# The last GEMM of a two-block transformer kernel: seven block products for eight

## The reference

```
def conv_ffn(h, w_up, conv_w, conv_b, w_down):
    u = causal_depthwise_conv(h @ w_up, conv_w, conv_b)
    gate, up = jnp.split(u, 2, axis=-1)
    return (jax.nn.silu(gate) * up) @ w_down
...
        x = x + conv_ffn(rms_norm_2(x, ffn_norm[layer]), ffn_w_up[layer], ffn_conv_w[layer],
                         ffn_conv_b[layer], ffn_w_down[layer])
```

## Time and profile before

| | |
|---|---|
| median of 3 runs | 1476.79 us |
| the profiled execution: span | 1474.6 us |
| around the span (median less span) | 2.2 us |
| TensorE busy | 1464.9 us, 99% |
| DVE, ACT, POOL busy | 824.7, 587.4, 207.0 us |
| mean granted TensorE clock | 0.998 |
| the stage of conv_down | from 1351.5 us to 1471.5 us of the span |

### The profile page before, as it was taken

One profiled execution on the slowest core, in us unless ns is written; L12 is line 12 of the kernel. 1 busy time (PEld: TensorE's weight loads), 2 busy tenths in 40 slices (PEclk: granted clock), 3 DMA queues, 4 the chain that ended last, 5 costly groups with the idle time before them and its releaser, 6 DMA issues.

```text
span 1474.6 us, 21796 instructions
## 1 busy us (share of the span) xinstructions
PE 1464.9 (99%) x8300; PEld 1221.1 (83%) x8300; DVE 824.7 (56%) x1264; ACT 587.4 (40%) x913; POOL 207.0 (14%) x193
## 2 busy tenths in 40 slices
...
GB/s 176 200 86 107 38 2 143 114 87 86 1 86 86 114 86 113 85 103 97 85 114 86 57 87 86 86 95 104 33 30 86 86 88 111 85 110 74 103 113 57
DMA packets 149743, 132.31 MB, mean 90 GB/s; under 512 B 6300, under 2 KB 133532, under 8 KB 149668
## 3 DMA queue, kind: packets, MB, share of 16 engines
...
q10 hardware_dynamic: 1056, 0.00, 0.0%
...
## 4 chain that ended last, share of the span: by engine, by line
PE 97%; DVE 1%; POOL 1%; DMA 0%; issue 0%; ACT 0%; SPq 0%; DVEq 0%; POOLq 0%
PE ps L2013 28%; PE ps L2015 28%; PE ps L2014 28%; PE ps L2448 3%; PE ps L2537 1%; PE ps L2555 1%; PE ps L2638 1%; PE ps L2647 1%; PE ps L2458 1%; PE ps L486 1%; POOL x_t L743 1%; DMA arena<-in_x 0%; PE ps L2479 0%; PE ps L2706 0%; PE ps L2707 0%; PE ps L2374 0%
## 5 line engine op out<-in xcount | busy, mean ns | idle before, releaser
L2013 PE MATMUL ps<-a_hi,w_hi 128*128 128x512 f32 (+2 forms) x1576 | 588.6, 373 | 3.7 <-DVE a_lo L1631 1.3
L2015 PE MATMUL ps<-a_hi,w_lo 128*128 128x512 f32 (+2 forms) x1576 | 583.3, 370 | 0.0
L2014 PE MATMUL ps<-a_lo,w_hi 128*128 128x512 f32 (+2 forms) x1576 | 583.1, 370 | 0.0
L819 ACT ACTIVATE w_hi<-raw 128x2048 fp32r<-128x2048 f32 x116 | 221.9, 1913 | 330.1 <-PE ps L2015 328.3
L2013 PEld LDWEIGHTS ps<-a_hi,w_hi 128*128 128x128 f32 (+1 forms) x1576 | 296.2, 188 | 60.1 <-DVE a_lo L1453 4.1
L1338 DVE TENSOR_TENSOR w_lo<-raw,w_hi 128x2048 fp32r<-128x2048 f32 x96 | 219.9, 2290 | 220.7 <-ACT w_hi L819 220.1
L2015 PEld LDWEIGHTS ps<-a_hi,w_lo 128*128 128x128 f32 (+1 forms) x1576 | 296.2, 188 | 51.9
L2014 PEld LDWEIGHTS ps<-a_lo,w_hi 128*128 128x128 f32 (+1 forms) x1576 | 296.3, 188 | 50.7 <-issue 0.7
L691 POOL TENSOR_TENSOR w_lo<-raw,w_hi 128x2048 fp32r<-128x2048 f32 x22 | 101.4, 4609 | 435.7 <-ACT w_hi L819 408.0
L1844 DVE TENSOR_TENSOR arena<-ps,rstd 128x512 f32<-128x512 f32 x88 | 60.1, 689 | 164.1 <-PE ps L2015 159.1
L2013 PE MATMUL ps<-w_hi,a_hi 128*128 128x512 f32 x368 | 144.0, 391 | 0.0
...
## 6 DMA issues: line engine op xcount, KB each, us to landing
raw<-in_w_gate_up SPq DMA_DIRECT2D x44, 512.0 KB, 4.7
raw<-in_ffn_w_up SPq DMA_DIRECT2D x44, 512.0 KB, 4.7
raw<-in_attn_w_in SPq DMA_DIRECT2D x36, 512.0 KB, 4.5
raw<-in_w_in SPq DMA_DIRECT2D x24, 512.0 KB, 4.7
raw<-in_w_down SPq DMA_DIRECT2D x22, 512.0 KB, 4.1
raw<-in_ffn_w_down SPq DMA_DIRECT2D x22, 512.0 KB, 3.9
raw<-in_w_mem_kv SPq DMA_DIRECT2D x16, 512.0 KB, 4.4
raw<-in_w_out SPq DMA_DIRECT2D x8, 512.0 KB, 4.0
```

The costliest lines, as they stand in the source:

```text
L819: act.activation(w_hi[:, ch.next_slot, :], raw[:, ch.next_slot, :], ACT.Copy).then_inc(weights_hi, 1)
L2013: pe.matmul(dst, s_hi, m_hi, start=start, stop=False, skip_group_check=across)
L2014: pe.matmul(dst, s_hi, m_lo, start=False, stop=False, skip_group_check=across)
L2015: return pe.matmul(dst, s_lo, m_hi, start=False, stop=stop, skip_group_check=across)
```

## The change

conv_down is replaced by a scheme after Strassen and Winograd. Of each pair of hidden tiles and its 256 rows of w_down, let A11, A12 be the first 256 tokens of the first and the second tile, A21, A22 the other 256 tokens, and W11, W12, W21, W22 the weights (first index the tile, second the half of the columns). With S1 = A21 + A22, S2 = S1 - A11, S3 = A11 - A21, S4 = A12 - S2, T1 = W12 - W11, T3 = W22 - W12, T2 = T3 + W11, T4 = W21 - T2 there are seven products in place of eight: P1 = A11 W11, P2 = A12 W21, P3 = S4 W22, P4 = A22 T4, P5 = S1 T1, P6 = S2 T2, P7 = S3 T3. The four quarters of the output are P1+P2, P1+P6+P5+P3, P1+P6+P7+P4 and P1+P6+P7+P5. Each product is 256 tokens by 512 columns over 128 of depth, and fills two PSUM banks.

Since PSUM has 8 banks, depth is run through twice (`STEPS`, 22 steps): steps 0 to 10 sum P1, P5, P7, P6 over the 11 pairs (24 matmuls a step), steps 11 to 21 then P2, P3, P4 on top of P1, P5, P7 in their banks (18 a step). At the turn ACT copies P1, P5, P7 out (`staged`), DVE adds P6 to P1 and that to three quarters (`join`), POOL adds P5 and P7 to one of them.

The work by engine: SP loads three quarters of w_down a step of the first run (256 KB each) and stores T2 to DRAM; in the second run it loads T2 and two quarters. The buffers are `raw`, `x_t` (free when the residual is turned) and a part of `arena` (free when the hidden matrix is whole). DVE makes T1 with T3 (128x1024), T2, T4 (128x512) and the weights' remainders (128x2048, then 128x1536). ACT makes all high parts. POOL makes S2 for each pair once (`basis`, two of 128x256, during conv_up), S1 and S3 or S4 (`sides`, 128x256) and the left operand's remainders (`sides_lo`), which were DVE's. Some semaphores of the start are joined into one (`x_norm`, `rel_moved`) with the same counts; the work there is the same. In `products` a triple is the first column of the side, the quarter and the first bank.

```diff
...
+        t2_dram = nc.dram_tensor("t2_dram", [FT // 2, 128, 512], F, kind="Internal").ap()
...
+        PAIRS_K = FT // 2
+        BUFFERS = (raw[:, :, :].rearrange("p a (q n) -> p (a q) n", n=512), x_t, region(16384, 8, 512))
...
+            def products(self):
+                if self.first:
+                    return ((512, 2, 0), (0, 0, 4), (256, 1, 6), (768, 3, 2))
+                return ((0, 1, 0), (512, 2, 4), (256, 0, 6))
+        STEPS = [Step(c) for c in range(2 * PAIRS_K)]
+        P1_BANK, P5_BANK, P7_BANK, P6_BANK = 0, 4, 6, 2
+        staged_1, staged_5, staged_7 = BUFFERS[0][:, 6:8, :], BUFFERS[1][:, 6:8, :], BUFFERS[2][:, 6:8, :]
...
+            def load_quarters(t):
+                if t.c == 0:
+                    sp.wait_ge(weights_split, TOTAL + CREDIT)
+                elif t.c == 1:
+                    sp.wait_ge(out_turned, KT)
+                elif t.c == 4:
+                    sp.wait_ge(hidden_written, 2 * CREDIT + 2 * FT)
+                else:
+                    sp.wait_ge(weights_split, TOTAL + CREDIT + t.before + 1)
+                if t.first:
+                    parts = ((2, 0, 0), (4, 0, 1), (5, 1, 1))
+                else:
+                    parts = ((1, 1, 0), (2, 1, 1))
+                    sp.wait_ge(t2_stored, 16 * (min(t.before, PAIRS_K - 1) + 1))
+                    sp.dma_start(t.q[:, 3, :], t2_dram[t.pair]).then_inc(rows_loaded[t.buffer], 16)
+                for to, k, n in parts:
+                    sp.dma_start(t.q[:, to, :], w_down[t.pair, k][:, n * 512:n * 512 + 512])\
+                      .then_inc(rows_loaded[t.buffer], 16)
+            def store_t2(t):
+                sp.wait_ge(quarter_sums, t.sums_done)
+                if t.c:
+                    sp.wait_ge(t2_stored, 16 * t.c)
+                sp.dma_start(t2_dram[t.pair], t.q[:, 3, :]).then_inc(t2_stored, 16)
+            load_quarters(STEPS[0])
+            load_quarters(STEPS[1])
+            for t in STEPS:
+                if t.first:
+                    store_t2(t)
+                if t.c + 2 < 4:
+                    load_quarters(STEPS[t.c + 2])
+                elif t.c == 2:
+                    load_quarters(STEPS[4])
+                    load_quarters(STEPS[5])
+                elif 3 <= t.c and t.c + 3 < len(STEPS):
+                    load_quarters(STEPS[t.c + 3])
...
+            def basis(t):
+                pool.wait_ge(hidden_written, 2 * CREDIT + FT + 2 * t.pair + 2)
+                a11, a21, a22 = t.hidden[:, 0:256], t.hidden[:, 256:512], t.hidden[:, 768:1024]
+                pool.tensor_tensor(a21, a21, a22, ALU.add).then_inc(basis_made, 1)
+                pool.wait_ge(basis_made, 2 * t.pair + 1)
+                pool.tensor_tensor(a21, a21, a11, ALU.subtract).then_inc(basis_made, 1)
+            def sides(t):
+                if t.c >= 3:
+                    pool.wait_ge(hidden_split, PAIRS_K + 2 * (t.c - 2))
+                pool.wait_ge(basis_made, 2 * (t.pair + 1))
+                a11, s2, a12, a22 = (t.hidden[:, n:n + 256] for n in (0, 256, 512, 768))
+                if t.first:
+                    pool.tensor_tensor(t.sums[:, 0:256], s2, a11, ALU.add).then_inc(side_sums, 1)
+                    pool.tensor_tensor(t.sums[:, 256:512], a22, s2, ALU.subtract).then_inc(side_sums, 1)
+                else:
+                    pool.tensor_tensor(t.sums, a12, s2, ALU.subtract).then_inc(side_sums, 1)
+            def sides_lo(t):
+                for n, (of, cols) in enumerate(t.side_parts()):
+                    pool.wait_ge(hidden_hi, PAIRS_K + 2 * t.c + n + 1)
+                    pool.tensor_tensor(t.side(a_lo)[:, cols], of, t.side(a_hi)[:, cols].bitcast(F), ALU.subtract)\
+                        .then_inc(hidden_split, 1)
+            for t in STEPS[:PAIRS_K - 1]:
+                basis(t)
+            sides(STEPS[0])
+            for t in STEPS:
+                if t.c == PAIRS_K - 4:
+                    basis(STEPS[PAIRS_K - 1])
+                if t.c + 1 < len(STEPS):
+                    sides(STEPS[t.c + 1])
+                sides_lo(t)
+                if t.c in (PAIRS_K + 5, PAIRS_K + 7):
+                    late = t.c - PAIRS_K - 5
+                    pool.wait_ge(product_joined, 4 + late // 2)
+                    pool.wait_ge(product_staged, 3)
+                    pool.tensor_tensor(out_quarter(1, 1), out_quarter(1, 1), staged_5 if late else staged_7, ALU.add)\
+                        .then_inc(product_joined, 1)
...
+            def sides_hi(t):
+                if t.c < 3:
+                    act.wait_ge(rows_free["conv_up"], t.c + 1)
+                elif t.c == 3:
+                    act.wait_ge(tile_done, G["conv_up"].signal_end)
+                else:
+                    act.wait_ge(tile_done, G["conv_up"].signal_end + t.c - 3)
+                for of, cols in t.side_parts():
+                    if of is t.sums:
+                        act.wait_ge(side_sums, t.sides_done)
+                    else:
+                        act.wait_ge(basis_made, 2 * (t.pair + 1))
+                    act.activation(t.side(a_hi)[:, cols], of, ACT.Copy).then_inc(hidden_hi, 1)
+            def quarters_hi(t):
+                act.wait_ge(quarter_sums, t.sums_done)
+                if t.c < 2:
+                    act.wait_ge(tile_done, G["conv_up"].signal_end - 2 + 2 * t.c)
+                else:
+                    act.wait_ge(tile_done, G["conv_up"].signal_end + t.c - 1)
+                act.activation(t.weight(w_hi), t.q[:, 0:t.many, :], ACT.Copy).then_inc(weights_hi, 1)
...
-                    first_rows_hi("conv_up", 2 * CREDIT + FT)
+                    sides_hi(STEPS[0])
+                    sides_hi(STEPS[1])
+                    quarters_hi(STEPS[1])
...
+                if ch.last_of_gemm:
+                    sides_hi(STEPS[2])
+                    quarters_hi(STEPS[2])
...
-            act.wait_ge(hidden_written, 2 * CREDIT + 2 * FT)
-            over_chunks(act, G["conv_down"], rows_hi)
+            for t in STEPS[3:]:
+                sides_hi(t)
+                if t.c == PAIRS_K + 1:
+                    staged(1, P1_BANK, staged_1)
+                    staged(2, P5_BANK, staged_5)
+                    staged(3, P7_BANK, staged_7)
+                quarters_hi(t)
...
+            def t1_and_t3(t):
+                loaded(t)
+                dve.tensor_tensor(t.q[:, 0:2, :], t.q[:, 4:6, :], t.q[:, 2:5:2, :], ALU.subtract).then_inc(quarter_sums, 1)
+            def t2(t):
+                dve.wait_ge(quarter_sums, t.sums_done - 1)
+                if t.before is not None:
+                    dve.wait_ge(t2_stored, 16 * (t.before + 1))
+                dve.tensor_tensor(t.q[:, 3, :], t.q[:, 1, :], t.q[:, 2, :], ALU.add).then_inc(quarter_sums, 1)
+            def t4(t):
+                loaded(t)
+                dve.tensor_tensor(t.q[:, 0, :], t.q[:, 1, :], t.q[:, 3, :], ALU.subtract).then_inc(quarter_sums, 1)
+            def quarters_lo(t):
+                dve.wait_ge(weights_hi, TOTAL + t.c + 1)
+                dve.tensor_tensor(t.weight(w_lo), t.q[:, 0:t.many, :], t.weight(w_hi).bitcast(F), ALU.subtract)\
+                   .then_inc(weights_split, 1)
+            def join(n):
+                dve.wait_ge(product_staged, 1)
+                if n == 0:
+                    dve.wait_ge(product_done, 4)
+                    dve.tensor_tensor(staged_1, staged_1, ps[:, P6_BANK:P6_BANK + 2, :], ALU.add).then_inc(product_joined, 1)
+                else:
+                    dve.wait_ge(product_joined, 1)
+                    to = out_quarter(*((0, 1), (1, 0), (1, 1))[n - 1])
+                    dve.tensor_tensor(to, to, staged_1, ALU.add).then_inc(product_joined, 1)
             def convolved(ch):
...
+                elif ch.last_of_gemm:
+                    t1_and_t3(STEPS[0])
+                    t2(STEPS[0])
+                    t1_and_t3(STEPS[1])
+                    t2(STEPS[1])
+                    quarters_lo(STEPS[0])
...
-                if ch.last_of_gemm:
-                    first_rows_lo(11)
...
+                if ch.last_of_gemm:
+                    t1_and_t3(STEPS[2])
+                    quarters_lo(STEPS[1])
+                    t2(STEPS[2])
...
+                if ch.last_of_gemm:
+                    t1_and_t3(STEPS[3])
+                    quarters_lo(STEPS[2])
+                    t2(STEPS[3])
...
-            over_chunks(dve, G["conv_down"], lambda ch: rows_lo(ch, 11))
             dve.wait_ge(out_copied, KT)
+            for t in STEPS[3:]:
+                after = STEPS[t.c + 1] if t.c + 1 < len(STEPS) else None
+                if after and after.first:
+                    t1_and_t3(after)
+                elif after:
+                    t4(after)
+                quarters_lo(t)
+                if after and after.first:
+                    t2(after)
+                if PAIRS_K + 1 <= t.c < PAIRS_K + 5:
+                    join(t.c - PAIRS_K - 1)
...
+            def seven_products():
```

(24 more changed lines are left out.)

133 lines of the change are left out of this document (79 added, 54 removed).

## The result

The changed kernel takes **1502.0 us** (1501.87 to 1502.99), the kernel before on the same chip 1476.8 (1476.51 to 1477.12): a ratio of 1.0173, 95% interval 1.0158 to 1.0187. The forecast was 1503, the range 1487 to 1515.

The account below looks back on a forecast made before the run. TensorE bounds the kernel before; after the change, DVE and POOL together. From 1350.3, 136.5 us of their work, 5 idle, 4.1 last step, 3.1 tail, 2 clock give span 1501.0; with 2.2 outside, 1503 us, range 1487 to 1515.

Parts of the forecast that it names:

- The products: Last stage: 462 matmuls in place of 528, 66 less by 0.2268 us, 15.0 us.
- The exclusion: Last stage: DVE and POOL operations reading two SBUF tensors exclude each other, an instruction at a time; matmuls wait.
- The sum: From DVE's first new split to its last: DVE 70.3 plus POOL 66.2 us, plus 5 us with neither working.
- the 0.58 us for 256 columns: Last stage: time a POOL operation of 256 columns excludes DVE, against 0.74 us shown.
- the 0.3 allowed: Program end after the last matmul: as long as before, 3.1 us, at most 0.3 us more.
- The waits: Last stage: TensorE waits for DVE's split or POOL's remainder at nearly every step; longest ahead of step 2, some 9 us.
- rival 1: Last stage: no exclusion, 15.0 us fewer matmuls plus the opening's waits; 1467 us, slower loads 1470; chance 0.06.
- The clock: Last stage: TensorE's clock falls after standing still; one or two unhidden falls, 2 us, bounds 0 and 8.
- Rival 3: Last stage: exclusion, and waits beyond 3 us lower the clock; six falls by 1.7 us, 10 us: 1513; chance 0.18.
- POOL's means: Last stage: POOL's 128x512 operations would average 2 us or more, against 1.30; staying at 1.3 would mean rival 1's time.
- Rival 2: Last stage: exclusion, but engines hide more in each other, say POOL never blocks DVE; 1470 us; chance 0.04.

Follow-up runs that it names:

- experiment 1: Changed kernel with GpSimd's two-input operations in the last GEMM replaced by memsets that read no SBUF: 1475.53 us, ratio 0.9989 to the kernel before.
- experiment 6: Changed kernel with GpSimd's two-input operations as memsets and another order at the turn into the last GEMM: 1467.36 us, ratio 0.9935 to the kernel before.
- experiment 8: Complete seven-product kernel with the left operand on VectorE (1474.30 us), only its sums given back to GpSimd: 1480.17 us, ratio 1.0021 to the kernel before.
- experiment 3: Changed kernel with one of the three matmuls of every product in the last GEMM left out: 1500.59 us, ratio 1.0161 to the kernel before.

## Why the prediction was right

**The products.** 66 matmuls fewer, 15.0 us: right, by the count.

**The exclusion.** Right, and it decides the result. Between the 1502.0 measured and the 1461.8 that 15.0 us off the kernel before would be lie 40.2 us. POOL's SBUF reads, taken away first, make up 26.5 of them (experiment 1), the order at the turn, once the pair is relieved, 8.2 (experiment 6), and 5.6 stay in that version, 3.4 of them as TensorE's waits for splits. (In the other sequence the shares differ: the order alone is worth 2.4.) A part of the shared time put back costs time again (experiment 8). The page that the prediction followed, "SBUF — State Buffer" of the Trainium skill (SBUF: two separate sides), also says that DVE's two-input operation contends only with a GpSimd operation that reads SBUF: the unhindered memsets, and the copy of one input that took 2.46 us beside a split, agree with both halves of that.

**The sum.** The first split was put at 1348.0 to 1350.3; it runs from 1348.01 to 1350.30. From there the two engines were to need 136.5 us and be idle together for 5: 1491.8. The last split ends here:

```profile
1489.37 2.13 DVE L2166 TENSOR_TENSOR w_lo<-x_t,w_hi 128x1536 fp32r<-128x1536 f32 x1 [2.04 <-ACT w_hi L1467]
1493.53 3.67 DVE L2248 TENSOR_TENSOR arena<-arena,ps 128x512 f32<-128x512 f32 x6 [2.02 <-PE ps L2258]
```
```profile
1496.06 0.39 PE L2258 MATMUL ps<-w_hi,a_lo 128*128 128x512 f32 x1
```

The last split ends at 1491.5. The stretches in which I find both without work (1375.6 to 1377.6, 1381.5 to 1382.3, 1387.5 to 1388.3, 1395.9 to 1396.3) add up to 4; between the first two POOL works while DVE waits for the load of step 4 (6.70 us in all). By experiment 8 the 0.58 us for 256 columns is good to 0.04. The mean step of the first run is 7.02 us from the split at 1396.33 to that at 1431.44 (7.38 by the terms), of the second 5.29 (4.58 and some 0.9 of joins and additions a step).

From there on luck helped. The span is 1500.1, only 0.9 below the forecast's 1501.0, but the forecast without its 2 us for the clock, 1499.0, is 1.1 too low. The last matmul ends at 1496.45 (second fence) where 1495.9 was forecast, since TensorE was still busy with the step before when the last split was made, and the end of the program takes 3.65 us in place of 3.1, more than the 0.3 allowed. These two, some 0.55 us each, stand where 2 us of clock were put.

**The waits.** Step 0 was put at 1353.2 (under rival 1), the wait ahead of step 2 at some 9 us:

```profile
1353.10 0.50 PE L2256 MATMUL ps<-w_hi,a_hi 128*128 128x512 f32 x1 [1.47 <-POOL a_lo L931]
...
1374.58 0.77 PE L2256 MATMUL ps<-w_hi,a_hi 128*128 128x512 f32 x1 [8.68 <-DVE w_lo L2166]
1385.91 0.76 PE L2256 MATMUL ps<-w_hi,a_hi 128*128 128x512 f32 x1 [4.02 <-DVE w_lo L2166]
```

"TensorE waiting at nearly every step" was too much: 12 waits of 22 steps by name. In part the slower matmuls stand in the waits' place: the 72 matmuls of steps 3 to 5 run from 1385.9 to 1405.2 without a wait, in 19.3 us for the 16.3 of full clock.

**The clock: the term that was mis-sized.** I had one or two falls that nothing hides, at 2 us. There were four. After the two long waits the granted clock was 0.51 and 0.50, the lower of the two levels (1.2 GHz); it fell again after waits of 2.59 us (ahead of the matmul at 1422.06) and 2.87 us (at 1467.42), and windows about these have 0.66 and 0.57:

```profile
1374.00:1378.00 4.00, 3.42 (x8) 0.51 0.31 102
1385.50:1391.00 5.50, 5.09 (x12) 0.50 0.57 192
1422.00:1427.00 5.00, 4.94 (x15) 0.66 0.38 108
1466.00:1474.00 8.00, 6.58 (x17) 0.57 0.49 163
```

The whole stage lost 12.9 us of matmul time, and nearly all of that cost nothing, because TensorE was not the bound: experiment 3 gives back only 1.4 us for 34.9 us of matmuls, and 1.36 of these are the last step's. So the term had too few falls and too high a price for them. Rival 3 (six falls that lengthen the stage by 10 us) has the lost matmul time nearly right and the price wrong; and its 3 us are no line that the rows draw, since two of the four falls follow shorter waits.

**POOL's means.** "2 us or more" for 128x512 was a little high; alone it is 1.30:

```profile
L931 POOL TENSOR_TENSOR a_lo<-arena,a_hi 128x512 fp32r<-128x512 f32 x22 | 40.4, 1837 | 0.0
```

**Rivals 1 and 2.** Rival 1, no exclusion in the kernel's own order, is what experiment 1 makes: 1475.5 us, and not the 1467 forecast. The 8.5 us are its opening. It was given 5.0 us of waits; TensorE waited 1.25, 2.70 and 4.09 us there, 8.0 in all, and lost some 4.5 us more to slower matmuls (110.0 us busy for 465 from 1351.7 on, where 105.5 are needed). Experiment 6 has rival 1's number, 1467.4, by luck: its order at the turn is another one. So without the exclusion the change would have won 0.1%, and not 0.7%. Rival 2's 1470 was not run; its ground, that POOL never blocks DVE, is against the rows: DVE's join of 1.22 us is shown with 2.31 behind a remainder.
